# A two-block network in fp32 on one core: inputs loaded at once, the key stage tile by tile, gate diagonals on ACT

## The reference, cut to what matters

```python
m_lat = jnp.split((silu(c) @ ada_w[l] + ada_b[l])[:, None, :], 6, axis=-1)   # ada_w: 1024 x 6144
m_ctx = jnp.split(silu(c_ctx) @ ada_w[l] + ada_b[l], 6, axis=-1)
h = modulate(rmsnorm(x, norm_mix[l]), m_lat[0], m_lat[1])      # h * (1 + scale) + shift
f, p, q, k, v, gates = split_proj(h @ w_in[l])                 # the same for the context, hc
x = x + m_lat[2] * merge(yf, yp, ya, gates, w_out[l])          # Fourier, pooling and attention branches
h2 = modulate(rmsnorm(x, norm_ffn[l]), m_lat[3], m_lat[4])
x = x + m_lat[5] * peer(h2, ...)                               # ctx too in layer 0

def peer(h, wq, sub_keys, u_tab, v_tab):
    q = (h @ wq).reshape(C, 8, 2, 128)                         # 8 heads x 2 sides = 16 queries of a token
    s = einsum('chpd,hpnd->chpn', q, sub_keys)                 # 128 keys for each
    s1, i1 = top_k(s[:, :, 0], 16); s2, i2 = top_k(s[:, :, 1], 16)
    top, pos = top_k(s1[..., :, None] + s2[..., None, :], 16)  # 16 picks of 16384 experts a head
    g = softmax(top)
    a = gelu(einsum('chkd,cd->chk', u_tab[eidx], h))
    return einsum('chk,chkd->cd', g * a, v_tab[eidx])          # 128 rows of u and 128 of v a token
```

## Time and profile before

| | us |
|---|---|
| median of 3 timed runs (lowest, highest) | 3696.3 (3693.75, 3699.58) |
| the profiled execution, its own time | 3679.2 |
| its span, first to last instruction | 3677.4 |
| PE busy | 2689.4 |
| DVE busy | 2342.6 |
| POOL busy | 1482.5 |
| ACT busy | 694.0 |

### The profile page before, as it was taken

The page is one execution under the profiler, slowest core; times in us unless marked ns, Lnnn a source line. Parts: engine busy times, 40 slices in busy tenths (PEclk is TensorE's granted clock), DMA queues, the critical chain, the costliest instruction groups (busy, mean ns, idle before and its releaser), DMA issues. The chain is left out here.

```text
span 3677.4 us, 30576 instructions
## 1 busy us (share of the span) xinstructions
PE 2689.4 (73%) x8773; PEld 1376.5 (37%) x8773; DVE 2342.6 (64%) x5334; ACT 694.0 (19%) x1885; POOL 1482.5 (40%) x1582
## 2 busy tenths in 40 slices
PE   6998676766697666863086886197417799999998
PEld 3445532223372232211022472042102265566555
DVE  1233877778876778789855468887886536433542
ACT  1021100312122200310022220022002213410341
POOL 0000365665546655676664006656666600000000
PEclk8999878986899878886599987599658999999999
DMA  8656699999999999999998349999999953234322
GB/s 307 240 194 225 248 403 389 352 360 333 400 360 369 355 395 403 363 370 360 370 368 311 105 151 378 407 387 381 383 407 364 362 207 132 92 138 141 141 92 75
DMA packets 345650, 1086.52 MB, mean 295 GB/s; under 512 B 32657, under 2 KB 41357, under 8 KB 338189
## 3 DMA queue, kind: packets, MB, share of 16 engines
q0 software_dynamic: 227216, 849.45, 60.4%
q1 hardware_dynamic: 118268, 235.12, 18.1%
HBM read 1080.21 MB, written 4.24 MB: 295 GB/s over the span
## 5 line engine op out<-in xcount | busy, mean ns | idle before, releaser
L2447 ACT ACTIVATE heads<-common,dots 128x128 f32<-128x128 f32 x768 | 277.9, 396 | 731.3 <-PE psum L2463 359.0
L1214 PE MATMUL psum<-ring,turned 128*128 128x512 f32 (+1 forms) x800 | 356.1, 598 | 75.0 <-issue 56.5
L2503 POOL DMA_INDIRECT lent<-in_peer_u_dram,picks_u x274 | 258.2, 942 | 351.2 <-DVE picks_u L2199 168.1
L2413 DVE SCALAR_TENSOR_TENSOR lent<-lent,psum 128x1024 f32<-128x1024 f32 x274 | 325.1, 1218 | 41.2 <-issue 20.5
L2463 PE MATMUL psum<-proj,heads 128*128 128x512 f32 x374 | 207.0, 655 | 181.4 <-DVE turned L2413 129.1
L2463 PE MATMUL psum<-lent,heads 128*128 128x512 f32 x524 | 285.6, 653 | 70.8 <-DMA lent<-in_peer_v_dram,picks_u 24.1
L2503 POOL DMA_INDIRECT lent<-in_peer_v_dram,picks_u x262 | 248.0, 947 | 133.8 <-issue 63.7
L1884 PE MATMUL psum<-ring,turned 128*128 128x512 f32 x512 | 243.1, 635 | 39.4 <-issue 13.4
L2421 DVE SCALAR_TENSOR_TENSOR psum<-lent,dots,psum 128x512 f32<-128x512 f32 x262 | 197.9, 755 | 101.4 <-DMA lent<-in_peer_v_dram,picks_u 55.0
L1214 PEld LDWEIGHTS psum<-ring,turned 128*128 128x128 f32 x800 | 161.5, 204 | 265.5 <-issue 253.3
L2413 DVE SCALAR_TENSOR_TENSOR proj<-proj,psum 128x1024 f32<-128x1024 f32 x195 | 232.7, 1218 | 37.7 <-issue 13.8
(11 more groups left out here) (416 smaller groups left out, 4698.3 us busy)
## 6 DMA issues: line engine op xcount, KB each, us to landing
ring<-in_w_in_dram SPq DMA_DIRECT2D x37, 2048.0 KB
ring<-in_peer_wq_dram SPq DMA_DIRECT2D x10, 2048.0 KB
...
proj<-in_ada_w_dram POOLq DMA_DIRECT2D x14, 1024.0 KB, 6.7
heads<-in_ada_w_dram POOLq DMA_DIRECT2D x13, 1024.0 KB, 7.1
gate_rows<-in_ada_w_dram POOLq DMA_DIRECT2D x13, 1024.0 KB, 7.1
...
```

The lines of the kernel that those rows point to most:

```text
L1214: mm = pe.matmul(psum[:, b % nb, 0:cols], lhs(k, it), w[:, kk, :], start=k == 0, stop=k == k_total - 1)
L2413: dve.scalar_tensor_tensor(out=src, in0=src, scalar=1.0, in1=kept_row, op0=ALU.mult, op1=ALU.mult, accum_out=weight).then_inc(rows_used.se ...
L2447: act.activation(diags[n % DIAGS], ident, ACT.Copy, scale=dots[:, j:j + 1]).then_inc(diag_ready.sem, 1)
L2503: pool.indirect_dma_start(out=row_slot(r), out_offset=None, in_=tables_dram[which], in_offset=bass.IndirectOffsetOnAxis(ap=picks_u[:, t, j ...
```

## The change

The inputs are issued in the set-up stage: x before the packs, ctx behind them, and then all three other modulation blocks, the fourth into a place of its own in `proj`. Squares, scaling and the transposes of the latents move into the set-up stage, and the small loads all go to the projection stage. The hosted pairs of modulation k-steps are put elsewhere. The key stages that aren't guests take one tile in each item, in the order `TILE_FIRST`; rows are turned back between items through PSUM banks 6 and 7; the last picks are made at the end of DVE's part of that stage, and POOL's rows go first into slots that are free there. The diagonals of the gates are made by ACT, between its copies, and DVE takes rows meanwhile.

```diff
+    beside_ring[len(plan) - 1] = (RING, proj[:, 0:SLOT], None, False)
...
+            if plan[n_load][0][0] == "ada":
+                turn = (turn + 1) % RING
...
             sp.dma_start(common, io["common"]).then_inc(*packs_loaded.one(16))
+            for t in range(2):
+                sp.dma_start(stream[:, t, :], io["x"][0, t * P:t * P + P, :]).then_inc(*latents_loaded.one(16))
...
+            for t in range(2):
+                sp.dma_start(stream[:, 2 + t, :], io["ctx"][0, t * P:t * P + P, :]).then_inc(*loaded.one(16))
             issue_loads(sp)
...
+                turn_raw(pe, 0)
...
+                scale_pair(dve, 0)
...
-                act.wait_ge(*step_v.at(7))
+                squares(act, latents_loaded, 0)
+                squares(act, loaded, 1)
+                act.wait_ge(*columns_known[0])
...
     def load_beside(sp):
-        load_inputs(sp)
-        small_queue.append(small_loads(sp))
-        sp.wait_ge(*loaded.now())
-        issue_loads(sp, islice(small_queue[0], 8), 3)
-        more_of_small(sp)
-    def more_of_small(sp):
-        for _ in islice(small_queue[0], 6):
+        issue_loads(sp)
+    def await_small(sp):
+        for _ in small_loads(sp):
...
+                if b == 2:
                     turn_raw(pe, 1)
...
+            for g in (0, 2):
                 dst, src = raw_part(g)
-                dve.wait_ge(*filled.at(g + 1))
+                dve.tensor_copy(dst, src).then_inc(*read_v.one())
+            scale_pair(dve, 1)
+            for g in (4, 6):
...
+            for s, k in [(0, k) for k in range(KD)] + [(1, k) for k in range(2)]:
+                x = turned_s[s][:, k, :]
+                dve.tensor_scalar(x, x, first_gain(0, k, s), first_shift(0, k, s), ALU.mult, ALU.add).then_inc(*step_v.one())
...
+            for k in range(2, KD):
...
-    def gates_of(gate_list, row0=0):
+    def gates_of(gate_list, source):
 
 
         diag = [soft[:, 128 * i:128 * i + 128] for i in range(3)]
         before = read_a.now()
 
         def tensor(pe):
-            if hosted():
-                pe.wait_ge(*before)
+            pe.wait_ge(*before)
             for i in range(len(gate_list)):
                 if i % 4 == 0:
                     yield 0
-                pe.wait_ge(*ready_v.at(i + 1))
+                pe.wait_ge(*ready_a.at(i + 1))
                 pe.matmul(psum[:, i // 4, 128 * (i % 4):128 * (i % 4) + 128], ones, diag[i % 3],
                           start=True, stop=True).then_inc(*products.one())
 
         def vector(dve):
-            for i, (w, s, k) in enumerate(gate_list):
-                if i >= 3:
-                    dve.wait_ge(*products.at(i - 2))
-                dve.tensor_scalar(diag[i % 3], ident, mods_v[:, 8 * (2 + 3 * w) + k, s:s + 1], None, ALU.mult).then_inc(*ready_v.one())
+            for _ in range(len(gate_list) // 4):
+                yield 2.2
 
         def scalar(act):
-            for q in range(len(gate_list) // 4):
+            def evict(q):
                 act.wait_ge(*products.at(4 * q + 4))
                 w, s, k = gate_list[4 * q]
                 act.copy(gate_row(w, s)[:, P * k:P * k + 512], psum[:, q, :]).then_inc(*read_a.one())
+            for i, (w, s, k) in enumerate(gate_list):
+                if i >= 3:
+                    act.wait_ge(*products.at(i - 2))
+                act.activation(diag[i % 3], ident, ACT.Copy, scale=source[:, 8 * (2 + 3 * w) + k, s:s + 1]).then_inc(*ready_a.one())
+                if i >= 5 and i % 4 == 1:
+                    evict(i // 4 - 1)
+            evict(len(gate_list) // 4 - 1)
...
+    TILE_FIRST = ((0, 0), (1, 0), (1, 1), (2, 0), (3, 0), (0, 1), (2, 1), (3, 1))
+    BLOCK_FIRST = ((0, 0), (1, 0), (2, 0), (3, 0), (3, 1))
...
+        order = BLOCK_FIRST if hosted() else TILE_FIRST
+        items = [(4 * b + j, t, 1 if (b, 1) in order else 2) for b, t in order for j in range(4)]
+        first_item = [4 * [b_ for b_, _ in order].index(b) for b in range(4)]
+        last_item = [4 * max(i for i, (b_, _) in enumerate(order) if b_ == b) + 3 for b in range(4)]
...
+        rows_at = [16 + 2 * n for n in range(len(rows_back))]
+        def turn_row_back(pe, n):
+            t, g = rows_back[n]
+            if n >= 2:
+                pe.wait_ge(*copied_back.at(n - 1))
+            for q in range(4):
+                mm = pe.transpose(psum[:, 6 + n % 2, q * P:q * P + P],
+                                  turned_s[s][:, 4 * g + q, (t % 2) * P:(t % 2) * P + P], ident)
+            mm.then_inc(*turned_back.one())
...
-                if h % 4 == 0 and t0 == 0:
-                    w = take(pe, ("wq", l, h // 4))
+                w = slot_view(n0 + h // 4)
+                if i == first_item[h // 4]:
+                    pe.wait_ge(*landing[n0 + h // 4])
                 yield 4 + asked_at(i)
                 pe.wait_ge(*(emptied if hosted() else read_v).at(4))
                 if i >= 3:
...
                     mm = pe.matmul(psum[:, i % 3, 0:P * nt], w[:, k, (h % 4) * P:(h % 4) * P + P],
                                    turned_s[s][:, k, P * t0:P * (t0 + nt)], start=k == 0, stop=k == KD - 1)
                 mm.then_inc(*products.one())
-                if h % 4 == 3 and t0 + nt == 2:
-                    release()
+                if i == last_item[h // 4]:
+                    freed[h // 4] = products.now()
                 if i >= 1:
                     dot(pe, i - 1)
+                if i in rows_at:
+                    turn_row_back(pe, rows_at.index(i))
             dot(pe, last)
-            turn_rows_back(pe)
+            used.extend(freed[b] for b in range(4))
...
+            if not hosted():
+                pair_indices(dve, 2 * s, PEER_HEADS - 2)
+                dve.wait_ge(*step_v.now())
+                write_picks(dve, l, 2 * s, 2 * TOPK, PICKS)
...
+                if i - 1 in rows_at:
+                    n = rows_at.index(i - 1)
+                    t, g = rows_back[n]
+                    act.wait_ge(*turned_back.at(n + 1))
+                    act.copy(mixed_v[:, t, 512 * g:512 * g + 512], psum[:, 6 + n % 2, :]).then_inc(*copied_back.one())
...
-    late_order = [0, 1, 2, 3, 11, 12, 4, 5, 10, 6, 7, 8, 9]
-    slot_no = ([r % ROWS for r in range(MORE_FROM)] + [(ROWS + r) % MORE_ROWS for r in range(THIRD - MORE_FROM)]
+    first_order = [6, 7, 8, 0, 1, 2, 3, 4, 5, 9]
+    late_order = [6, 7, 8, 11, 12, 0, 1, 2, 3, 4, 5, 10, 9]
...
-    def rows_beside_keys(pool, wq0, rows):
+    def rows_beside_keys(pool, wq0, after_lent, after_products, rows):
 
         pool.wait_ge(*picked_first.now())
-        pool.wait_ge(*used[wq0])
         for row in range(rows):
-            issue_row(pool, rows_used.total + row, 0, 0, row)
-        begun[0] = rows
-    def rows_beside_picks(pool, keys_done, rows):
-        pool.wait_ge(*keys_done)
-        for row in range(begun[0], rows):
+            if row == after_lent:
+                pool.wait_ge(*used[wq0])
+            if row == after_products:
+                pool.wait_ge(*products.now())
...
-        quads.host(project_, (1, 3, 5, 7))
+        quads.host(project_, (1, 3, 5, 7, 11))
         quads.host(branch, (0,))
         quads.host(merge, (1, 5, 9, 13, 17))
         quads.host(turn)
-        quads.host(attend, (4, 18))
+        quads.host(attend, (4, 11, 18))
         quads.host(merge_late, (1, 3))
         turn, out_, norm, keys = to_keys(0, 0, True)
         quads.host(turn, (0,))
-        quads.host(out_, (1, 3))
-        quads.host(norm, (0,))
+        quads.host(out_, (1, 2, 3))
+        quads.host(norm)
         wq0 = len(used) + 1
-        quads.host(keys, (3, 8), then_rows=lambda pool: rows_beside_keys(pool, wq0, 4))
-        keys_done = products.now()
-        quads.host(lambda: last_picks(0, 0), then_rows=lambda pool: rows_beside_picks(pool, keys_done, 9))
+        quads.host(keys, then_rows=lambda pool: rows_beside_keys(pool, wq0, 3, 7, 9))
...
-        quads.host(keys, then_rows=lambda pool: rows_beside_keys(pool, wq0_, 6))
-        keys_done_ = products.now()
-        quads.host(lambda: last_picks(1, 0), then_rows=lambda pool: rows_beside_picks(pool, keys_done_, 12))
+        quads.host(keys, then_rows=lambda pool: rows_beside_keys(pool, wq0_, 5, 9, 12))
```

134 lines of the change are left out of this document (53 added, 81 removed).

## The result

The changed kernel took 3728.8 us in the median of 5 runs (3720.2 to 3735.3), the kernel before 3699.6 beside it: a ratio of 1.0065, with a 95% interval of 1.004 to 1.009 (all ratios here are those on record; they are worked out from the single runs and differ a little from the quotient of two medians, which is 1.0079 here). It is slower; the forecast was 3683 (3667 to 3695). Three more groups of runs gave 1.0049 [1.0029, 1.0069], 1.0053 [1.0034, 1.0072] and 1.0067 [1.0051, 1.0084].

What follows compares the result with a forecast made beforehand. DMA bytes at 403 GB/s bound the expert stages, serial stages the rest. Start, pairs and norm (+3.9), layer 0's keys and gates (-13) and layer 1 (-4.5) gave -13.6 us from 3696.3: 3683, range 3667 to 3695.

Steps and rivals of the forecast that it cites:

- The start: Set-up to projection: inputs and modulation blocks issued without a DMA hole, projection starting at 39.0 against 50.16, -11.1 us.
- first pair +2.4: Projection: the first modulation pair's blocks queue beside weights and tables, so its second half waits 2.4 us longer.
- The pairs: Modulation pairs moved into projection, attention and output stages, some waiting for their second block: +13.7 us.
- +6.0 at the branch: Projection's end and branch stage: two close pairs, the second waiting for its block, +6.0 us, two thirds of it waiting.
- T0: Layer 0's first key product, 336.04 us in the kernel before; forecast to move by +3.9 us.
- Key stage, layer 0: One-tile items, picks finished there: the copy opening the expert stage at T0+70.5 rather than +78.8.
- The gates: First expert stage: ACT makes 24 diagonals while rows continue; together with layer 0's key stage -13 us from T0.
- Layer 1: Layer 1's key stage: copy at T0'+75.3 against +76.8, three more rows gathered, -4.5 us.
- T0': Layer 1's first key product, at 2131.48 us in the kernel before.
- starved pairs: Rival: POOL's modulation blocks land in 9 to 12.3 us, five close pairs wait +24 us more, 3707 us; chance 0.07.
- the head start is taken back: Rival: expert-stage guests wait for their weights anyway, only the copies' shifts stay, -5.9 us, 3690 us; chance 0.18.
- The 358 GB/s a core: Rival: by the skill's HBM read bandwidth the gain at the gates falls by 7.2 us, -6.4, 3690 us; chance 0.04.

Runs made afterwards that it cites:

- experiment 11: The changed kernel, with rows gathered beside the key stages waiting until the fourth query block has landed: ratio 1.0024.
- experiment 6: The kernel before with the modulation pairs moved and the key stage changed, start and gates as before: ratio 1.0041, fast pace.
- experiments 2 and 3: The changed kernel with gate diagonals back on DVE: 1.0010; the kernel before with only the gate diagonals moved to ACT: 1.0045.
- experiments 13 and 14: The changed kernel without 11 rows beside ACT's diagonals; the changed kernel with POOL pausing after 27 rows until ACT's gate work ends: both 1.0012.
- experiment 18: The changed kernel with POOL pausing after 27 rows until the gate stage's ACT work is done, at the slow pace: 1.0072.

## Why the prediction was wrong

**The start** was right in its first number (39.0 forecast, 39.59 measured) and in the cause, the hole. What failed is the term behind it, first pair +2.4: 5.9 us were lost there, in the changed kernel (third group of products 4.7 us earlier, 64.72 against 69.41) as in the start alone. I let the pair's 2 MB move at half the rate beside weights and tables. They were issued at 40.0 and 40.6, and the second landed at 54.7, 14.1 us later, in queues that moved 400 GB/s from 39 to 55.

**The pairs.** The mechanism, a pair that waits for its block, was right and mis-sized: +6.0 at the branch became +10.3 by the merge stage (from -4.7 to +5.6). I took the landing of 5.3 us of the earlier trace rows. It was 7.7, since SP issues a block of 2 MB at 98.6 just ahead of POOL's; and PE, idle for 5.45 us, came back at a granted clock of 0.50, which is 1.2 GHz, 1.94 us for 8 products. Attention and late merge cost 4.0 for 2.3. Output, norm and the keys' transposes cost 2.5 where I had 4.3. Together 22.7 against 15.0 from the projection's start, so T0 is +12.1, not +3.9.

**Key stage, layer 0.** "3.7 MB land at about T0+34.7 against a need at T0+34.2: 0.5 us" failed: PE waited 3.36, as late as T0+37.6. A part of it was arithmetic: at the 403 GB/s that the sum uses elsewhere, 3.7 MB take 9.2 us from T0+26.6, which is 1.6 us late and not 0.5. The rows beside the block are the cause of the wait, since with rows that come behind it the wait is gone (experiment 11). The copy came at T0+75.3 for +70.5: 3.4 us won, below my lower bound of 8.3. Its place varies, +71.2 to +75.3 in the four profiles of the changed kernel; at the fast pace, in experiment 6, it is +69.6 against +76.4, 6.8 us won.

**The gates** hold the step that decided. I wrote that "DVE keeps taking rows and POOL keeps gathering", counted the rows as won, and priced only the 2.5 us by which ACT outlasts them. The sum had some 5 us of gain here beyond the copy's shift. The bytes did flow, 410 GB/s from 434 to 446, but the runs show a loss of 14 to 17 us at the slow pace: undoing ACT's gates gives 0.4% of the 0.5 to 0.65% back, and adding them to the kernel before costs as much (experiments 2 and 3). Two things came that the sum did not have. ACT's chain of diagonals, forecast at 13.0 us, took 31, so the guests started 21 us later than with DVE's gates. And the rows were not free: DVE's order is fixed, and the second tile's picks, which had 24 rows of slack, now stand behind all 256 rows of the first tile. POOL waits 10.3 to 13.4 us for them in the slow profiles, and this wait appears in no kernel whose gates give no rows.

How the 14 to 17 us divide between the two is not shown. The late picks alone cost nothing that can be told at the fast pace (experiments 13 and 14). Cutting the stage at the slow pace from 31.7 to 18.8 us won nothing (experiment 18), but the pause that cut it kept POOL idle for 11.2 us. And no kernel with the whole of ACT's gates and unpaused rows ran at the fast pace, so the changed kernel's ratio there stays open too.

The Trainium skill, "ScalarE: Activation LUTs", Rules for kernel authors, would have multiplications on VectorE. The runs side with it here (1.0010 against 1.0049), though not by its price of an ACTIVATE, which the trace bears out (0.40 us). At that price the loss would be a stage of 13 us instead of 12; the rule would not have told the size.

**Layer 1** was forecast at -4.5 and cost 2.8 (experiment 6): the late block again (PE waits 1.3 to 6.1 us for it in the profiles), and rows that are gathered earlier but start no stage earlier. With rows that wait for the block, the copy comes 3.7 us earlier than before at the slow pace, at T0'+73.1, and 0.9 earlier at the fast one.

**The rivals.** The one on the slower side, starved pairs, has the right place and sign and about a third of its price: it asked for 24 us more than mine and got 7.7 (22.7 against 15.0). That the head start is taken back was part of the truth. None had the gates as a loss, and my range left 0.08 to everything slower. The 358 GB/s a core that I took from the Trainium skill, "DMA: Bandwidth & Descriptors", Bandwidth, are given there for both cores of a memory domain streaming, which I left out. This stretch, of one core, has 410 over 12 us.

## What to carry to other kernels

Where one engine's program interleaves two kinds of work in a fixed order, work given to it "for free" is put ahead of all that follows on it; ask what stands last in that queue and how much slack it has (24 rows here, all of it used up). A head start of 11 us was worth 4, since the queues were full behind it: count the bytes that must land by each wait, not the time at which a stage begins. And a load that others need at a known time is issued first: rows that were only meant to fill the queues cost about 0.3% by delaying one 2 MB block in each layer.

## What the runs showed of the chip

Two paces of the same program, 3571 and about 3700 us, and the difference shows as idle time named issue on PE, ACT and DVE (340, 445 and 133 us against none) and named remote, not as longer instructions (DVE is busy for 2342.6 us in the slow profile and 2342.4 in the fast one). At the slow pace ACT made one diagonal in 4 to 5.6 us while POOL issued a gather every 1.25 us, at 114 GB/s as at 410, and ran on within 5 us of POOL's last issue. No packet of the profile's instruction queues moved between 440 and 470 us in the changed kernel, so the stops don't end with a load of instructions. What passes between the two engines, and why it begins after the eighth diagonal, these runs don't tell.
